# Six places for split weight slabs in the expert passes, and splits issued four slabs ahead of their use

## The reference, cut to what matters

```python
def moe_swiglu(h, router_w, wg, wu, wd):
    logits = (h @ router_w).astype(jnp.float32)
    probs = jax.nn.softmax(logits, axis=-1)
    top_p, top_i = lax.top_k(probs, TOP_K)
    ...
    for e in range(N_EXPERTS):
        out = out + comb[..., e:e + 1] * swiglu(h, wg[e], wu[e], wd[e]).astype(jnp.float32)

def swiglu(h, wg, wu, wd):
    return (jax.nn.silu(h @ wg) * (h @ wu)) @ wd
```

## Time and profile before

| | |
|---|---|
| runs | 2147.92, 2150.46, 2150.85 us; median 2150.46 |
| profiled execution | its span, from the first to the last instruction, is 2145.6 us |
| busy share of the span | PE 95%, PEld 91%, DVE 61%, ACT 39%, POOL 10% |
| expert passes | 8, about 1497 to 2112 us of the span |
| in six of them (1575.00 to 2032.58 us) | DVE 373.23 of 457.58 us busy, ACT 258.17, PE 441.06; granted clock 1.00 |
| weight loads | 489 of 512 KB, median 4.2 us from issue to landing |

### The profile page before, as it was taken

How to read it: one execution, slowest core, us unless ns; L and a number is a source line. 1 busy time by engine, 2 the same in 40 slices (tenths; PEclk the granted TensorE clock), 3 DMA queues, 4 the chain that set the end, 5 groups by cost and what they waited for, 6 DMA issues and landing times.

```text
span 2145.6 us, 38756 instructions
## 1 busy us (share of the span) xinstructions
PE 2045.9 (95%) x15539; PEld 1942.3 (91%) x15539; DVE 1307.6 (61%) x1973; ACT 847.3 (39%) x1202; POOL 209.1 (10%) x343
## 2 busy tenths in 40 slices
PE   7999999999999999999999999995999999999996
PEld 7999899999999999999989999994888888888875
DVE  5563446675545552345643466654888788888877
ACT  4312223443433222233122234433555555555544
POOL 0002231010000000000022310102000000000011
PEclk9999999999999999999999999996999999999997
DMA  5232248567222223222332475623677777777775
GB/s 181 80 121 87 91 131 281 163 188 278 89 92 96 88 90 97 90 90 85 115 101 77 159 261 172 188 87 126 216 248 243 236 250 247 232 255 244 241 264 188
DMA packets 108638, 352.38 MB, mean 164 GB/s; under 512 B 14168, under 2 KB 18328, under 8 KB 108248
## 3 DMA queue, kind: packets, MB, share of 16 engines
q1 hardware_dynamic: 87464, 278.46, 40.1%
q0 software_dynamic: 21056, 72.21, 10.2%
HBM read 304.80 MB, written 46.27 MB: 164 GB/s over the span
## 4 chain that ended last, share of the span: by engine, by line
PE 70%; DVE 11%; DMA 7%; issue 6%; ACT 5%; POOL 1%; ACTq 0%; SPq 0%; DVEq 0%; POOLq 0%
PE ps L1875 53%; PE ps L1869 6%; DVE w_lo L1154 5%; PE ps L2186 5%; ACT w_hi L781 3%; DMA raw<-slabs 3%; PE ps L2200 2%; PE ps L2188 2%; PE ps L2206 1%; DVE gsum L1751 1%; DVE usum L1762 1%; DMA C_s<-Cs 1%; DMA Cs<-ml_C 1%; DVE ma_parts L1792 1%; DVE yt L1787 0%
## 5 line engine op out<-in xcount | busy, mean ns | idle before, releaser
L1154 DVE TENSOR_TENSOR w_lo<-raw,w_hi 128x1024 fp32r<-128x1024 f32 x487 | 597.4, 1227 | 284.0 <-ACT w_hi L781 281.7
L781 ACT ACTIVATE w_hi<-raw 128x1024 fp32r<-128x1024 f32 x488 | 508.6, 1051 | 419.0 <-PE ps L1875 376.2
L1875 PE MATMUL ps<-h_hi,w_hi 128*128 128x260 f32 x2544 | 524.1, 287 | 26.1 <-DVE h_lo L1163 13.7
L1875 PE MATMUL ps<-h_hi,w_lo 128*128 128x260 f32 x2544 | 513.2, 283 | 0.0
L1875 PE MATMUL ps<-h_lo,w_hi 128*128 128x260 f32 x2544 | 512.4, 283 | 0.0
L1875 PEld LDWEIGHTS ps<-h_hi,w_hi 128*128 128x128 f32 x2544 | 394.5, 189 | 41.4 <-DVE w_lo L1154 26.9
L1875 PEld LDWEIGHTS ps<-h_hi,w_lo 128*128 128x128 f32 x2544 | 392.9, 189 | 0.0
L1875 PEld LDWEIGHTS ps<-h_lo,w_hi 128*128 128x128 f32 x2544 | 392.2, 189 | 0.0
L2186 PE MATMUL ps<-hg,w_hi 128*128 128x320 f32 x1408 | 375.0, 349 | 14.5 <-DVE w_lo L1154 12.1
L2188 PE MATMUL ps<-hg,w_lo 128*128 128x160 f32 x1408 | 334.9, 238 | 0.0
L2186 PEld LDWEIGHTS ps<-hg,w_hi 128*128 128x128 f32 x1408 | 266.3, 189 | 33.3 <-DVE w_lo L1154 22.3
(11 more groups left out here) (365 smaller groups left out, 2554.0 us busy)
## 6 DMA issues: line engine op xcount, KB each, us to landing
raw<-slabs SPq DMA_DIRECT2D x489, 512.0 KB, 4.2
gates_kept<-sq SPq DMA_DIRECT2D x64, 260.0 KB, 2.3
gs<-gates_kept POOLq DMA_DIRECT2D x64, 260.0 KB, 3.6
token_slots<-zeros POOLq DMA_DIRECT2D x1, 9600.0 KB, 34.9
rows_in<-token_slots POOLq DMA_DIRECT2D x9, 512.0 KB, 4.3
Cs<-ml_C POOLq DMA_DIRECT2D x8, 512.0 KB, 6.5
kb<-mlstm_key_query_rows POOLq DMA_DIRECT2D x8, 512.0 KB, 7.8
qb<-mlstm_key_query_rows POOLq DMA_DIRECT2D x8, 512.0 KB, 9.0
```

What stands on the lines that cost most here:

```text
L781: nc.scalar.activation(w_hi[:, n % SPL], raw[:, place(n)], ACT.Copy).then_inc(hi_ready, 1)
L1154: tt_op(w_lo[:, n % SPL], raw[:, place(n)], w_hi[:, n % SPL].bitcast(F32), ALU.subtract).then_inc(lo_ready, 1)
L1875: ins = mm(out[:, hf], wgt_part[:, slot, tile], in_part[:, kk, HALF * hf:HALF * (hf + 1)], start=first and not ends and in_part is in_hi, ...
```

## The change

The parts of split slabs get six places in the expert passes: the three of before and three more in `w_hi_more` and `w_lo_more`, which lie where the normed activations `h_hi` and `h_lo` lay (the router is the last to read those). The first 18 slabs of a pass rotate through six places, the last 15 through five (`SPLIT_PLACE`), and `split_hi` waits for the slab that last had the place (`split_place_freed`). In `expert_pass`, ACT and DVE split the slab four places ahead of PE's gate slab instead of two, and slabs 2 and 3 of the first pass are split before the loop. Waits, products and loads are otherwise the same; `RAW` and `JOB_PLACE` stay.

```diff
+SPLIT_PLACES = 6
+SPLIT_AHEAD = 4
+SPLIT_PLACE = [i % SPLIT_PLACES for i in range(3 * SPLIT_PLACES)] + [
+    i % (SPLIT_PLACES - 1) for i in range(S_JOB - 3 * SPLIT_PLACES)]
+
+def split_place(n):
+
+    if n < MOE0:
+        return n % SPL
+    at = SPLIT_PLACE[(n - MOE0) % S_JOB]
+    return (MOE0 + at) % SPL if at < SPL else at
+
+def split_place_freed(n):
+
+    if n < MOE0 + SPL:
+        return n - SPL + 1
+    i = n - MOE0 + S_JOB
+    after = MOE0 - S_JOB + 1 + max(m for m in range(i) if SPLIT_PLACE[m % S_JOB] == SPLIT_PLACE[i % S_JOB])
+    return max(after, MOE0) if n == MOE0 + SPL else after
...
-    h_hi = sb("h_hi", [P, KT, T], F32R)
-    h_lo = sb("h_lo", [P, KT, T], F32R)
+    normed = ExitStack()
+    h_hi = sb("h_hi", [P, KT, T], F32R, where=normed)
+    h_lo = sb("h_lo", [P, KT, T], F32R, where=normed)
+    normed.close()
+    w_hi_more = sb("w_hi_more", [P, SPLIT_PLACES - SPL, KT, P], F32R)
+    w_lo_more = sb("w_lo_more", [P, SPLIT_PLACES - SPL, KT, P], F32R)
...
             if n >= SPL:
-                act.wait_ge(slab_done, j * turn(n) + (n - SPL + 1))
-            nc.scalar.activation(w_hi[:, n % SPL], raw[:, place(n)], ACT.Copy).then_inc(hi_ready, 1)
+                act.wait_ge(slab_done, j * turn(n) + split_place_freed(n))
+            nc.scalar.activation(high_part(n), raw[:, place(n)], ACT.Copy).then_inc(hi_ready, 1)
...
             nc.scalar.activation(comb[:], comb[:], ACT.Exp).then_inc(wt.sem, 1)
+            split_hi(MOE0 + 3)
...
-            last = FE_TILES - 1
             for f in range(FE_TILES):
-                if f > 1:
-                    split_hi(s0 + gate_slab(f) + 2, j)
-                elif f == 0:
+                ahead = s0 + gate_slab(f) + SPLIT_AHEAD
+                if f:
+                    split_hi(ahead, j)
+                else:
                     nc.scalar.activation(msig[0:1, 0:1], eps[0:1], ACT.Sigmoid).then_inc(table_loaded, 1)
-                    split_hi(s0 + gate_slab(f) + 3, j)
                 act.wait_ge(m_sum, f0 + (f + 1))
                 if f == 0:
                     act.wait_ge(table_loaded, j + 1)
                 nc.scalar.activation(msig[:], gsum[:], ACT.Sigmoid).then_inc(m_sig, 1)
-                if f > 1:
-                    split_hi(s0 + gate_slab(f) + 3, j)
-                if f == 0:
-                    split_hi(s0 + down_slab(0), j)
-                elif f < last:
-                    split_hi(s0 + down_slab(f - 1) + 2, j)
+                split_hi(ahead + (1 if f else 0), j)
+                split_hi(ahead + (2 if f else 1), j)
                 act.wait_ge(m_act, f0 + (f + 1))
                 nc.scalar.activation(ma_parts[:, f % 2, 0:CAP], ma[:, f % 2], ACT.Copy).then_inc(m_hi, 1)
-                if f == 0:
-                    split_hi(s0 + down_slab(0) + 1, j)
-            split_hi(s0 + down_slab(last - 1) + 2, j)
             gathered_hi(j + 1, 1)
             gathered_hi(j + 1, 0)
-            split_hi(s0 + down_slab(last) + 2, j)
-            split_hi(s0 + 2, j + 1)
+            split_hi(s0 + S_JOB + SPLIT_AHEAD - 1, j)
```

More of the change, by code:

```diff
@@ L170, in decoder @@
     x = sb("x", [P, KT, T])
-    h_hi = sb("h_hi", [P, KT, T], F32R)
-    h_lo = sb("h_lo", [P, KT, T], F32R)
+    normed = ExitStack()
[4 more added lines that the diff above has]
+    w_lo_more = sb("w_lo_more", [P, SPLIT_PLACES - SPL, KT, P], F32R)
+    sb("beside_more", [P, 2 * KT * (T - (SPLIT_PLACES - SPL) * P)])
     raw = sb("raw", [P, RAW, KT, P])
@@ L432, in decoder, with high_part, low_part @@
     block = ctx.enter_context(nc.Block())
+    def high_part(n):
+        at = split_place(n)
+        return w_hi[:, at] if at < SPL else w_hi_more[:, at - SPL]
+    def low_part(n):
+        at = split_place(n)
+        return w_lo[:, at] if at < SPL else w_lo_more[:, at - SPL]
     def evac(o, j=0):
@@ L1153, in split_lo @@
             dve.wait_ge(hi_ready, j * turn(n) + (n + 1))
-            tt_op(w_lo[:, n % SPL], raw[:, place(n)], w_hi[:, n % SPL].bitcast(F32),
+            tt_op(low_part(n), raw[:, place(n)], high_part(n).bitcast(F32),
                   ALU.subtract).then_inc(lo_ready, 1)
@@ L1744, in expert_pass @@
             s0, f0 = MOE0, j * FE_TILES
-            last = FE_TILES - 1
             for f in range(FE_TILES):
-                if f > 1:
-                    split_lo(s0 + gate_slab(f) + 2, j)
+                ahead = s0 + gate_slab(f) + SPLIT_AHEAD
+                if f:
+                    split_lo(ahead, j)
                 dve.wait_ge(slab_done, j * S_JOB + (s0 + gate_slab(f) + 1))
@@ L1752, in expert_pass @@
                 if f == 0:
-                    split_lo(s0 + 2, j)
-                    split_lo(s0 + gate_slab(f) + 3, j)
+                    split_lo(ahead, j)
                 dve.wait_ge(m_sig, f0 + (f + 1))
                 tt_op(ma[:, f % 2], gsum[:], msig[:], ALU.mult).then_inc(m_gate, 1)
[L1757 to L1760, removed]
+                if f:
+                    split_lo(ahead + 1, j)
                 dve.wait_ge(slab_done, j * S_JOB + (s0 + gate_slab(f) + 2))
@@ L1764, in expert_pass @@
                 tt_op(ma[:, f % 2], ma[:, f % 2], usum[:], ALU.mult).then_inc(m_act, 1)
[L1765 to L1770, removed]
+                split_lo(ahead + (2 if f else 1), j)
                 lo_of_act(f, f0)
@@ L1773, in expert_pass @@
                     add_rest(j + 1)
-                    split_lo(s0 + down_slab(0) + 1, j)
-            split_lo(s0 + down_slab(last - 1) + 2, j)
             gathered_lo(j + 1, 1)
             gathered_lo(j + 1, 0)
-            split_lo(s0 + down_slab(last) + 2, j)
+            split_lo(s0 + S_JOB + SPLIT_AHEAD - 1, j)
             dve.wait_ge(slab_done, j * S_JOB + (s0 + S_JOB))
@@ L1853, in _ @@
                 shares()
+                split_lo(MOE0 + 2)
+                split_lo(MOE0 + 3)
                 nc.vector.memset(rank[:], 0.0).then_inc(y_main, 1)
@@ L2185, in gate_or_up @@
                 for kk in range(KT):
-                    mm(out[:, 0:2 * CAP], w_hi[:, (s0 + s) % SPL, kk], hg[:, kk], start=kk == 0,
+                    mm(out[:, 0:2 * CAP], high_part(s0 + s)[:, kk], hg[:, kk], start=kk == 0,
                        stop=False, skip_group_check=True)
-                    ins = mm(out[:, 0:CAP], w_lo[:, (s0 + s) % SPL, kk], hg[:, kk, 0:CAP],
+                    ins = mm(out[:, 0:CAP], low_part(s0 + s)[:, kk], hg[:, kk, 0:CAP],
                              start=False, stop=kk == KT - 1, skip_group_check=True)
@@ L2196, in down @@
                 pe.wait_ge(m_lo, 2 * (f0 + (f + 1)))
-                parts, slot_n = ma_parts[:, f % 2], (s0 + s) % SPL
-                for a, (at, w) in enumerate(((0, w_hi), (0, w_lo), (CAP + REST, w_hi))):
+                parts, w_high, w_low = ma_parts[:, f % 2], high_part(s0 + s), low_part(s0 + s)
+                for a, (at, w) in enumerate(((0, w_high), (0, w_low), (CAP + REST, w_high))):
                     for hf_ in range(2):
-                        mm(ps[:, 4 + hf_], parts[:, at:at + P], w[:, slot_n, 4 * hf_:4 * hf_ + 4],
+                        mm(ps[:, 4 + hf_], parts[:, at:at + P], w[:, 4 * hf_:4 * hf_ + 4],
                            start=f == 0 and a == 0, stop=f == FE_TILES - 1 and a == 2)
@@ L2203, in down @@
                     pe.wait_ge(y_added, j + 1)
-                for a, w in enumerate((w_hi, w_lo)):
+                for a, w in enumerate((w_high, w_low)):
                     for hf_ in range(2):
                         ins = mm(ps[0:2 * REST, 6 + hf_], parts[:, P:CAP + REST],
-                                 w[:, slot_n, 4 * hf_:4 * hf_ + 4],
+                                 w[:, 4 * hf_:4 * hf_ + 4],
                                  start=f == 0 and a == 0, stop=f == FE_TILES - 1 and a == 1)
```

## The result

The changed kernel is slower: 2175.6 us (median of four runs, 2169.14 to 2179.85) against 2149.19 for the kernel before, ratio 1.0126, 95% interval 1.0112 to 1.0140. The ratio is worked out from all runs and is not the quotient of the two medians, which would be 1.0123. Forecast was 2153.9, with 2143 to 2164 as the range.

What follows compares the result with a forecast made beforehand. DVE's chain of gate sums was taken to fill the pass (76.5 us forecast, 76.26 before). Eight passes +1.9, ahead of the first pass +2.5, end -1.0: +3.4 us on 2150.46, so 2153.9; range 2143 to 2164.

Steps and rivals of the forecast that it cites:

- Tile 0: First hidden tile of a pass, gate sum 0 to 1 on DVE: 7.9 us, where before had 9.49.
- mid tiles: DVE's six intervals from tile 1 to tile 7: unchanged at 6.33 us each, 38.0 together.
- the end of the kernel: One low part fewer ahead of the last results' copies: -1.0 us.
- Tiles 7 to 10: Three intervals where three places of `raw` hold what four held: mean 6.83 us each, 20.5 together.
- PE's waits for `w_lo` gone and waits for the activation in their place: Sign expected in the changed profile: PE waits for the activation instead of for low parts of slabs.
- Last tile to the next pass ... Sum 10.1: Last gate sum of a pass to the next pass's first: 10.1 us, where before had 9.25.
- a rival with 0.07: Pauses ahead of down(10) drop the clock to 1.2 GHz, costing 2.3 to 4.6 us a pass: 2172 to 2191 us, chance 0.07.
- the 2.12 us at which the clock had stayed: Argument against the clock's fall: the longest gap at clock 1.00 was 2.12 us, and the clock stayed at 1.00.
- The other argument against the rival, that the transposes break the pause: Argument against the clock's fall: transposes of the gathered tokens interrupt PE's pause ahead of down(10).
- The 5.27 us from gate sum to activation: Part of the 10.1 us sum: last gate sum to the activation's split, taken as in a mid tile, 5.27 us.
- The term ahead of the first pass: Two more loads, 1.05 MB, delay the scatter and POOL's first gather: +2.5 us, between 0 and 3.6.
- The places were the bound: Rival: PE's 4.3 us of pauses a pass vanish with more places, giving 2118 us, chance 0.06.

Runs made afterwards that it cites:

- Experiment 2: Changed kernel plus matmuls that nobody reads, before and after the transposes in the last hidden tile, filling PE's pauses: 2161.51 us, ratio 1.0059.
- experiment 3: Changed kernel with the four places of raw in even order (0, 1, 2, 0, 3, 1, 0, 2, 3) for a pass's last nine slabs: 2142.52 us, ratio 0.9977.
- experiment 1: Changed kernel with slab 35's split in the last hidden tile moved behind the activation's split and the gathered tokens: 2155.72 us, ratio 1.0036.
- experiment 4: Changed kernel with the first pass's early splits of slabs 2 and 3 moved behind the first gathered tokens: 2167.47 us, ratio 1.0093.
- experiment 5: Kernel before with the six places for split slabs and their waits, but its old order of splits: 2145.59 us, ratio 0.9996.
- Experiments 7 and 9: 7: changed kernel, even order of raw, ACT's first two high parts ahead of the sigmoid, ratio 0.9870; 9: both edits in the kernel before, ratio 0.9940.

## Why the prediction was wrong

Most of the sum was right. Tile 0 took 8.0 (7.9 forecast), mid tiles 6.33, and the end of the kernel gained 0.9 (1.0). Tiles 7 to 10 took some 20.6 (20.5), but that agreement is luck: the sum had three intervals of 6.83, and measured were 6.3, 7.2 and 7.1. "PE's waits for `w_lo` gone and waits for the activation in their place" is what the waits show.

**The step that failed is "Last tile to the next pass ... Sum 10.1".** It measured 13.0 on average, 2.9 more, so 20.6 us in seven passes. Two things are missing in it, the clock with some 1.6 to 2 us and a late slab with 1.1.

*The clock.* The sum took down(10) at 2.41 us, full clock. That fall of the clock was a rival with 0.07, its time, 2172 to 2191, holds the result, and the range left it out. Experiment 2 puts its price at 11 to 14 us, 1.6 to 2 a pass, and the first pass of experiment 3 at 1.55 (11.52 against 9.97, with the activation's split at 4.87 us in both); the rival had 2.3 to 4.6. So it is in part luck that the rival's time holds the result: the late slab made up for what its price had too much. I held the 2.12 us at which the clock had stayed against it as if that length were the test; experiment 1 shows 1.65 us followed by a fall and 2.46 by none. Nor did the clock always stay at that place: in the profiled execution of the changed kernel, whose code there is the same, PE pauses for only 1.81 us, and the clock falls (0.83 over 10 us):

```profile
1252.23 0.48 PE L1897 MATMUL ps<-h_hi,w_hi 128*128 128x260 f32 x2 [1.81 <-DVE sq L1505]
...
1250.00:1260.00 10.00, 8.19 (x56) 8.01 (x55) 9.84 (x11) 1.22 (x2) 1.06 (x2) 0.83 0.86 299
```

The other argument against the rival, that the transposes break the pause, failed as well: they lay between the pauses of 2.38 and 2.30 us, and the clock fell. The prediction had already worked out that 4.5 us of pause would lie almost in one place, and 0.07 was too little for that.

*The late slab.* The 5.27 us from gate sum to activation were a mid tile's, with slabs that were there. In the last tile the split ahead of the activation is that of slab 35, the last of the stretch with three places, and in five of the seven passes its load was late: the activation's split started 6.0 to 6.8 us behind the gate sum there, 4.9 to 5.1 in the other two. On average it started at 6.01 us, where the sum has 5.27 - 0.39 = 4.88: the 1.1 us a pass. I charged the three places for the intervals 7 to 10, but they bind one tile later. The first slab whose place was used only three slabs before is 27, and its split is the last one ahead of the gate sum of tile 8 (the interval from tile 7 is 6.3 us, without delay); slabs 28 to 33 lie in the next two intervals (7.2 and 7.1), and 34 and 35 stand in the last tile, where I forgot them.

Experiment 3 ties both to one cause. With the even order the last tile took 9.97 us against the 10.1 of the sum, and the clock held from the second pass on (it fell in the first, where the interval behind tile 7 was 7.1 us even so). So the sum's last tile describes the kernel without that stretch of three places, and what it missed was a bill of the same stretch, paid at the end of the pass. This is shown by taking the stretch away; that PE's lead makes the first pause is read from rows, where 1.6 us of tiles stand against 1.6 us of pause. What decides between a fall and none after pauses of like length stays open.

The term ahead of the first pass measured +4.0 us in the place of +2.5. The cause was right: experiment 4 takes back 3.1 to 3.2, inside the bound of 3.6 from the window's 288 GB/s. The remaining 0.8 to 0.9 is not shown to come from the loads; among the profiled executions with the early splits the first gather starts from 1489.8 to 1492.5 us, without them from 1486.7 to 1489.0.

The rival "The places were the bound" fell with experiment 5. The page "Perfetto Trace Analysis" of the Trainium skill, section "Optimization Strategy", says that consistent bubbles can mean too few buffers. The runs do not bear that out here: twice as many buffers alone left PE's waits as they were (15.3 us in the rows of experiment 5, 15.5 before; ratio 0.9996). Experiments 7 and 9 show where the places do count: in an order of ACT's work that they allow.

## What to carry to other kernels

Here more buffers helped only through the order that they make possible. So sum each engine's in-order list first, and use new slack for the waits in it (here a high part ahead of the sigmoid: 0.9870 against 0.9977). Work that is moved ahead of a chain must be ready by then, so follow its load as well, above all where fewer places are in use. And where a stage's waits are gathered into one place ahead of TensorE, count what the clock then takes, as a case and not as a footnote.

## What was not expected of the hardware

The clock fell to 1.2 GHz after a pause of 1.65 us in one pass and held after 2.46 in another pass of the same kernel. At one place of unchanged code it held after 2.12 us in one execution (granted clock 1.00) and fell after 1.81 in another (0.83 over 10 us). A fall cost 1.4 to 2.0 us in down(10) (3.8 to 4.43 us instead of 2.4) in the changed kernel, and some products in PE's pauses, with no use of their own, avoided it (granted clock 1.00).
